# Softmax sums of two attentions inverted by one VectorE reciprocal instead of a logarithm, an exponential and a refinement

## The chip, the cores and the metric

One core of a Trainium2 chip. The metric is the device time of one execution in microseconds (us), the median of several runs; lower is better. Engines: TensorE (PE, matmul; PEld its weight load), VectorE (DVE), ScalarE (ACT), GpSimd (POOL), SyncE (SP, which issues the transfers here).

## The reference

One step of a one-layer encoder over 1024 new prompt frames and 32 sample frames (1056 in all, width 1024): a SwiGLU block, a mixer, a second SwiGLU block, a last norm. The mixer has three groups of columns: a gated convolution, a forgetting attention (8 heads of 64) and a cross-attention over 256 memory tokens (4 heads of 64). Both attentions end in a softmax:

```python
def _mem_attention(q, k, v):
    s = jnp.einsum('bqhd,bkhd->bhqk', q, k).astype(F32) * (HEAD_DIM ** -0.5)
    p = jax.nn.softmax(s, axis=-1)
    return jnp.einsum('bhqk,bkhd->bqhd', p.astype(v.dtype), v)
```

The forgetting attention adds a difference of running sums of log forget values to the logits and masks later keys. Everything is in 32-bit floats. The outputs of the three groups are joined, multiplied by `w_out` and added to x.

## The kernel before, in words

Everything is kept transposed: 128 rows of features by 1056 columns of frames. A matrix product in full precision is three matmuls on parts of each operand (high times high, high times low, low times high; lines 277 to 279). The program is written out by hand for each engine: each engine has its own list of instructions in order, and waits on semaphores that count finished instructions. `A["mixed"]` counts the VectorE instructions that scale the attention's output; TensorE, ScalarE and SP wait for it.

Heads go in pairs of 64 + 64 rows. There are four forgetting pairs (`attend(g)`, about 840 to 1170 us) and two memory pairs (`mem_pairs`, about 1170 to 1271 us), one after the other; then the product with `w_out` (`out_product`) begins. For a pair TensorE makes q, k and v, ScalarE and VectorE norm and split them, TensorE makes scores by row for the row maxima (VectorE, `smax` or `mem_smax`), then scores by key (`keyed`), of which ScalarE takes the exponential (`exps`), then the weighted sum of values (`weigh`, lines 2766 and 3016).

The values of a head stand beside a block of ones of 64 columns (`VO`, `v_and_ones`). So a weighted sum fills a PSUM bank in which 64 rows hold the head's output and the other 64 rows hold the softmax sum, already repeated for every row. Each pair has six such banks, called parts here (x = 0 to 5): for each head two of 512 frames and one of 32.

Each part is scaled as follows. ScalarE (`sum_rough`, lines 1453 and 1455, or `mem_sum_rough`, lines 1619 and 1621) takes the logarithm of the sum from PSUM, then the exponential of its negative: a rough inverse in `lr` (`sum_r0`). VectorE (`mixed`, lines 2217, 2219, 2224, or `mem_mixed`, lines 2314, 2316, 2321) multiplies it by the sum, refines it, and multiplies the output by it into `mixf`. There is one `lr` and one `lt`, so ScalarE waits for the scaling of part x - 1 before it starts on part x.

What stands around it in the order of the engines:

- ScalarE, forgetting pair: `sum_rough(x)` comes among the 28 exponentials, three blocks after the part's last one; copies of turned row maxima (`maxima`, line 1434) follow it.
- VectorE, forgetting pair: all 18 row maxima, then the six parts, then the next pair's head norm (line 1706).
- VectorE, memory pairs: part 0 to 5 of the first pair have row maxima of the second pair between them (`mem_smax(1, ...)`, line 2305); then come two remainders (`mix_lo`, line 2154), and part 0 to 5 of the second pair with a remainder behind each. A remainder is the low part of a row block of the joined output, which `out_product` reads.
- TensorE: a part's bank is free for the next use only after its scaling. In the memory pairs the sums of parts 3, 4 and 5 of the first pair wait for parts 1, 0 and 2 (`mem_bank_free`, line 2991), those of the second pair for parts 3, 4, 5 of the first, and its own part 5 for its own part 2. The output products wait for the banks of the second pair (line 3055).
- SP stores `mixf` after the sixth part of each pair (line 895; line 911 for the first memory pair) and loads the rows back later; `memory_gain` (line 2143) writes over `mixf` after that store.
- ScalarE and VectorE between the fourth forgetting pair and the memory: squares of the memory tokens (line 1518), the tokens' scale (`memory_scaled`, lines 2250 and 2254), the first query's norm, the memory gains (line 2143), for which TensorE waits before its third product (`mp["dve"]`, line 2953).

Of the kernel before, what the change touches and what calls it, by code (L numbers as in the profile page):

```python
# [22 lines left out]
P = 128  # L23
# [8 lines left out]
def hybrid_step(nc, i, o):  # L32
# [31 lines left out]
    with ctx:  # L64
# [120 lines left out]
        lr = sb("sum_r0", [P, 512], F32, xs)  # L185
        lt = sb("sum_rs", [P, 512], F32, xs)
# [48 lines left out]
        def semaphores(tag, names):  # L235
# [14 lines left out]
                       "qhi qlo tturned tcopied scores smax mturned mcopied keyed expd pv rough_sum mixed stored")  # L250
# [185 lines left out]
        def mem_rows(p, i):  # L436
# [5 lines left out]
                         mcopied=5, keyed=MB, expd=MB, pv=MB, rough_sum=12, mixed=18, stored=48)  # L442
# [3 lines left out]
                         mturned=5, mcopied=5, keyed=NB["fox"], expd=NB["fox"], pv=NB["fox"], rough_sum=12, mixed=18,  # L446
# [153 lines left out]
        def _(sp):  # L600
# [283 lines left out]
            for g, (kind, it) in enumerate(ATTEND):  # L884
                v = ITER["conv"] + g
                load_mixer(v + 1)
                store_tokens(g)
                if g + 1 < NG:
                    load_minusF(g + 1)
                    load_cached(g + 1)  # L890
                else:
                    load_mixer(MEMV + 1)
                    load_mem_cached(0)
                sp.wait_ge(A["mixed"], 18 * g + 18)
                store_mix(v)
# [15 lines left out]
            sp.wait_ge(A["mixed"], mem(0, "mixed", 18))  # L911
# [153 lines left out]
        def _(act):  # L1065
# [309 lines left out]
            def last_mix_hi():  # L1375
                act.wait_ge(A["mixed"], mem(1, "mixed", 18))
                act.activation(hh[:, KT - 1, :], mixf[:, :], ACT.Copy).then_inc(MIX["hi_last"], 1)

            def attend(g):
# [116 lines left out]
                done = 0  # L1496
                for n in range(NB[kind]):
                    exps(n)
                    if n == max(V_BEHIND):
                        v_copy(8)  # L1500
                    if n == V_TURNED:
                        tokens(5)
                        tokens(6)
                    if done < 6 and n >= PARTS[kind][done][0] + 3:
                        sum_rough(done)
                        done += 1
# [3 lines left out]
                for x in range(done, 6):  # L1510
                    sum_rough(x)
# [97 lines left out]
            def mem_sum_rough(p, x):  # L1609
                w = mem_block(p, 2 * x)[5]  # L1610
                r = half_rows(1 - x // 3)
                act.wait_ge(A["pv"], mem(p, "pv", 2 * x + 2))
                if x:
                    act.wait_ge(A["mixed"], mem(p, "mixed", 3 * x))
                elif p:
                    act.wait_ge(A["mixed"], mem(0, "mixed", 18))
                else:
                    act.wait_ge(A["mixed"], 18 * NG)
                act.activation(lr[r, 0:w], bank(MEM_OUT[p][x], w)[r], ACT.Ln).then_inc(A["rough_sum"], 1)
                act.wait_ge(A["rough_sum"], mem(p, "rough_sum", 2 * x + 1))  # L1620
                act.activation(lr[r, 0:w], lr[r, 0:w], ACT.Exp, scale=-1.0).then_inc(A["rough_sum"], 1)

            def mem_pairs():
# [34 lines left out]
                for n in range(MB):  # L1658
# [5 lines left out]
                    if n in (4, 6, 8, 10):  # L1664
                        mem_sum_rough(0, n // 2 - 2)
                    if n in (8, 10, 11):
                        mem_maxima(1, (8, 10, 11).index(n))
                mem_sum_rough(0, 4)
                mem_sum_rough(0, 5)
                for n in range(MB):  # L1670
                    mem_exps(1, n)
                    if n in (1, 3):
                        mem_maxima(1, 3 + n // 2)
                    if n in (4, 6, 8, 10):
                        mem_sum_rough(1, n // 2 - 2)
                mem_sum_rough(1, 4)
                mem_sum_rough(1, 5)
# [17 lines left out]
        def _(dve):  # L1695
# [460 lines left out]
            def attend(g):  # L2156
# [54 lines left out]
                def mixed(x):  # L2211
# [97 lines left out]
            def mem_mixed(p, x):  # L2309
# [3 lines left out]
                dve.wait_ge(A["rough_sum"], mem(p, "rough_sum", 2 * x + 2))  # L2313
                dve.tensor_tensor(lt[l, 0:w], PS[l, b:b + w], lr[l, 0:w], ALU.mult).then_inc(A["mixed"], 1)
                dve.wait_ge(A["mixed"], mem(p, "mixed", 3 * x + 1))
                dve.scalar_tensor_tensor(lt[r, 0:w], lt[l, 0:w], -2.0, lr[l, 0:w], ALU.add, ALU.mult)\
                   .then_inc(A["mixed"], 1)
                dve.wait_ge(A["mixed"], mem(p, "mixed", 3 * x + 2))
                if x == 0:
                    dve.wait_ge(MIX["stored"], 16 * (MEMV + p))  # L2320
                dve.scalar_tensor_tensor(mixf[r, s:s + w], PS[r, b:b + w], -1.0, lt[r, 0:w], ALU.mult, ALU.mult)\
                   .then_inc(A["mixed"], 1)
# [63 lines left out]
        def _(pe):  # L2386
# [220 lines left out]
            def attend(g):  # L2607
# [4 lines left out]
                def head_sums(m):  # L2612
# [7 lines left out]
                    elif g and m == 1:  # L2620
                        pe.wait_ge(A["mixed"], 18 * (g - 1) + 9)
# [8 lines left out]
                def bank_free(n):  # L2630
# [6 lines left out]
                    elif g and b in (0, 1, 4, 5):  # L2637
                        pe.wait_ge(A["mixed"], 18 * (g - 1) + {0: 12, 1: 6, 4: 15, 5: 18}[b])
# [115 lines left out]
                def weigh(n):  # L2754
# [7 lines left out]
                    if q0 == SEQ and first:  # L2762
                        pe.wait_ge(A["cv_loaded"], 32 * g + 32)
                        if j:
                            pe.wait_ge(A["mixed"], 18 * g + 3)
# [177 lines left out]
            def mem_product(p, n):  # L2943
# [6 lines left out]
                if p == 0 and n < 2:  # L2950
                    pe.wait_ge(A["mixed"], 18 * (NG - 1) + (6 if n else 12))
# [18 lines left out]
                if (p, n) == (0, 1):  # L2970
                    pe.wait_ge(A["mixed"], 18 * NG)
# [19 lines left out]
            def mem_bank_free(p, x):  # L2991
# [5 lines left out]
                elif p == 0:  # L2997
                    pe.wait_ge(A["mixed"], mem(0, "mixed", (6, 3, 9)[x - 3]))
                elif x < 3:
                    pe.wait_ge(A["mixed"], mem(0, "mixed", (12, 15, 18)[x]))  # L3000
                elif x == 5:
                    pe.wait_ge(A["mixed"], mem(1, "mixed", 9))
# [45 lines left out]
            def out_product(c, d, ks):  # L3048
# [5 lines left out]
                elif ks[0] == 0 and OBANK[d] in (0, 1, 2, 6, 7):  # L3054
                    pe.wait_ge(A["mixed"], mem(1, "mixed", {0: 12, 1: 6, 2: 3, 6: 18, 7: 15}[OBANK[d]]))
# [60 lines left out]
```

## Time and profile before

| | |
|---|---|
| median of 3 runs | 2103.62 us (2102.03 to 2103.83) |
| the profiled execution | 2104.28 us, span 2102.5 us |
| mean granted TensorE clock | 0.988 of full speed |
| TensorE, VectorE, ScalarE, GpSimd busy | 2030.8, 1307.0, 991.0, 451.3 us |
| forgetting pairs | about 840 to 1170 us from the span's start |
| memory pairs | about 1170 to 1271 us |

The profile shows one execution; times count from the span's start. A row of an engine gives the line of the kernel, the operation, out<-in, shapes and durations; in brackets stands for how long the engine was idle before it and what ended that. The product with `w_out` and the two SwiGLU blocks fill most of the rest with matmuls.

### The profile page before, as it was taken

Reading aid. Unit: us, or ns where it says so; the run is one execution under the profiler, and the core shown is the slowest. Engines: PE = TensorE matmul, PEld = TensorE weight load, DVE = VectorE, ACT = ScalarE, POOL = GpSimd, SP = SyncE. Lnnn points to the kernel's source line nnn. Section 1 sums busy time; section 2 is a strip of 40 time slices with the busy share of each in tenths; the row PEclk is TensorE's granted clock in tenths of the full one; section 3 lists DMA queues with packets and bytes.
Section 4 is the critical chain, followed back from the end, with each engine's and each line's share of the span. In section 5 each row is a group of like instructions: output and inputs, shape, how many; then the busy total and the mean of one; then the engine's idle time right before and its main releaser. Section 6 shows DMA issues by size and latency. Waiting matters only on the chain.

```text
span 2102.5 us, 35729 instructions
## 1 busy us (share of the span) xinstructions
PE 2030.8 (97%) x14062; PEld 1935.1 (92%) x14062; DVE 1307.0 (62%) x2087; ACT 991.0 (47%) x1689; POOL 451.3 (21%) x225
## 2 busy tenths in 40 slices
PE   5999999999999999999999979989999999999998
PEld 5999999999999999776877858979999999999997
DVE  7999657983425763645645664589975588723323
ACT  6556344564334431455555652265543456433423
POOL 0000000004666643011012332000000000166662
PEclk8999999999999999999999989999999999999999
DMA  7554324555755447321122133055432265485742
GB/s 230 135 145 132 92 63 143 164 150 186 240 181 188 136 133 51 89 77 46 53 77 54 48 137 130 1 174 160 134 102 82 85 182 162 128 274 173 236 140 113
DMA packets 296853, 274.52 MB, mean 131 GB/s; under 512 B 29864, under 2 KB 238888, under 8 KB 296432
## 3 DMA queue, kind: packets, MB, share of 16 engines
q1 hardware_dynamic: 296688, 272.25, 43.5%
q8 instruction: 113, 1.85, 0.4%
q14 instruction: 52, 0.43, 0.1%
HBM read 222.41 MB, written 49.80 MB: 129 GB/s over the span
## 4 chain that ended last, share of the span: by engine, by line
PE 88%; DVE 5%; ACT 4%; issue 1%; another core or an unknown queue 0%; DVEq 0%; ACTq 0%
PE banks L277 27%; PE banks L278 27%; PE banks L279 26%; PE banks L2766 3%; DVE scores_minusF L2208 1%; PE banks L2734 1%; PE banks L2735 1%; PE banks L2688 1%; ACT k_hi_twice L1400 1%; PE banks L3016 0%; DVE head_rstd L1710 0%; DVE head_rstd L1706 0%; DVE head_rstd L1708 0%; ACT head_r L1088 0%
## 5 line engine op out<-in xcount | busy, mean ns | idle before, releaser
L277 PE MATMUL banks<-hforms_hi,w_hi 128*128 128x264 f32 x2112 | 602.6, 285 | 18.5 <-DVE hforms_lo L1910 9.6
L278 PE MATMUL banks<-hforms_lo,w_hi 128*128 128x264 f32 x2112 | 602.9, 285 | 0.0
L279 PE MATMUL banks<-hforms_hi,w_lo 128*128 128x264 f32 x2112 | 601.5, 285 | 0.0
L968 POOL TENSOR_TENSOR w_lo<-w_raw,w_hi 128x1024 fp32r<-128x1024 f32 x132 | 321.9, 2443 | 1203.2 <-ACT w_hi L1196 1203.2
L277 PEld LDWEIGHTS banks<-hforms_hi,w_hi 128*128 128x128 f32 x2112 | 399.5, 189 | 22.1 <-issue 7.2
L279 PEld LDWEIGHTS banks<-hforms_hi,w_lo 128*128 128x128 f32 x2112 | 398.9, 189 | 0.0
L278 PEld LDWEIGHTS banks<-hforms_lo,w_hi 128*128 128x128 f32 x2112 | 398.5, 189 | 0.1
L277 PE MATMUL banks<-acts_a,w_hi 128*128 128x352 f32 x960 | 309.9, 323 | 0.0
L279 PE MATMUL banks<-acts_a,w_lo 128*128 128x352 f32 x960 | 309.2, 322 | 0.0
L278 PE MATMUL banks<-acts_a,w_hi 128*128 128x352 f32 x960 | 309.0, 322 | 0.0
L1196 ACT ACTIVATE w_hi<-w_raw 128x1024 fp32r<-128x1024 f32 x132 | 139.5, 1058 | 283.1 <-PE banks L279 259.3
L277 PE MATMUL banks<-h_hi,w_hi 128*128 128x352 f32 x576 | 199.6, 347 | 4.8 <-DVE vT L2143 3.0
L279 PE MATMUL banks<-h_hi,w_lo 128*128 128x352 f32 x576 | 187.0, 325 | 0.0
L278 PE MATMUL banks<-h_lo,w_hi 128*128 128x352 f32 x576 | 186.8, 324 | 0.0
L277 PEld LDWEIGHTS banks<-acts_a,w_hi 128*128 128x128 f32 x960 | 180.3, 188 | 0.2
L278 PEld LDWEIGHTS banks<-acts_a,w_hi 128*128 128x128 f32 x960 | 180.3, 188 | 0.2
L279 PEld LDWEIGHTS banks<-acts_a,w_lo 128*128 128x128 f32 x960 | 180.2, 188 | 0.0
L1130 ACT ACTIVATE w_hi<-w_raw 128x512 fp32r<-128x512 f32 x228 | 142.7, 626 | 55.7 <-PE banks L279 53.9
L1130 ACT ACTIVATE w_hi<-w_sums 128x1024 fp32r<-128x1024 f32 x112 | 118.6, 1059 | 87.6 <-PE banks L279 78.5
L1804 DVE TENSOR_TENSOR w_lo<-w_raw,w_hi 128x512 fp32r<-128x512 f32 x228 | 155.8, 683 | 0.1
L1927 DVE TENSOR_TENSOR acts_a<-acts_f,acts_a 128x704 fp32r<-128x704 f32 x60 | 107.1, 1795 | 59.0 <-ACT acts_a L1184 58.9
L1813 DVE TENSOR_TENSOR w_lo<-w_sums,w_hi 128x1024 fp32r<-128x1024 f32 x112 | 136.4, 1218 | 0.4
(338 smaller groups left out, 3557.4 us busy)
## 6 DMA issues: line engine op xcount, KB each, us to landing
w_raw<-in_w_ffn_down SPq DMA_DIRECT2D x132, 512.0 KB, 3.8
w_raw<-in_w_ffn_gate SPq DMA_DIRECT2D x76, 512.0 KB, 5.4
w_raw<-in_w_ffn_up SPq DMA_DIRECT2D x76, 512.0 KB, 5.2
act_rows<-act_f SPq DMA_DIRECT2D x44, 528.0 KB, 2.9
acts_f<-act_rows SPq DMA_DIRECT2D x66, 352.0 KB, 4.1
w_raw<-in_w_in SPq DMA_DIRECT2D x20, 512.0 KB, 5.7
x_spill<-xT SPq DMA_DIRECT2D x4, 2112.0 KB, 8.5
xT<-x_spill SPq DMA_DIRECT2D x6, 1408.0 KB, 9.3
```

The source lines that it names most:

```text
L277: eng.matmul(out, w_hi, x_hi, start=first, stop=False, skip_group_check=added)
L278: eng.matmul(out, w_hi, x_lo, start=False, stop=False, skip_group_check=added)
L279: return eng.matmul(out, w_lo, x_hi, start=False, stop=last, skip_group_check=added)
L968: pool.tensor_tensor(wlo[:, wd_slot(e), :], raw[:, wd_slot(e), :], whi[:, wd_slot(e), :].bitcast(F32), ALU.subtract)\
L1130: act.activation(slots(whi, wxh, G[q], n), src, ACT.Copy).then_inc(f[f"{which}_hi"], 1)
L1196: act.activation(whi[:, wd_slot(e), :], raw[:, wd_slot(e), :], ACT.Copy).then_inc(f["wd_hi"], 1)
L1400: act.activation(KS1[half_rows(j), j, s:s + w], kT[half_rows(j), s:s + w], ACT.Copy)\
L1804: dve.tensor_tensor(slots(wlo, wxl, slot, 1), r[:, at:at + 1, :], slots(whi, wxh, slot, 1).bitcast(F32), ALU.subtract).then_inc(f[f"{which ...
L1813: dve.tensor_tensor(slots(wlo, wxl, slot, 2), SS[:, 2 * part:2 * part + 2, :], slots(whi, wxh, slot, 2).bitcast(F32), ALU.subtract)\
L1927: dve.tensor_tensor(acts(p)[:, 1, :, :], astg[:, m % 4, :, :], acts(p)[:, 0, :, :].bitcast(F32), ALU.subtract).then_inc(f["act_lo"], 1)
L2208: dve.tensor_tensor_reduce(junk[0:rows, 0:w], PS[0:rows, b:b + w], nF[0:rows, j, k0:k0 + w], 1.0, -3e38, ALU.add, ALU.max, m).then_inc(A[" ...
L2766: pe.matmul(PS[:, 512 * ob + oc:512 * ob + oc + w], VO[0:kr, vo, j, :], PRT[0:kr, (b0 + n) % 4, 0:w], start=first, stop=last, skip_group_c ...
```

## The change

One VectorE reciprocal per part takes the place of ScalarE's two instructions and VectorE's first two. It reads the sums from PSUM and writes their inverse into the output's rows of `lt`, which has two halves used in turn. The part's wait is for TensorE's last weighted sum (`A["pv"]`) in place of ScalarE's. ScalarE's `sum_rough` and `mem_sum_rough` and their waits are gone; `lr` is gone. `A["mixed"]` counts two instructions per part instead of three, and every wait on it is renumbered to the same part.

```diff
-        lr = sb("sum_r0", [P, 512], F32, xs)
-        lt = sb("sum_rs", [P, 512], F32, xs)
+        lt = sb("one_over_sums", [P, 2, 512], F32, xs)
...
-                def sum_rough(x):
-                    n, j, b, w, s = PARTS[kind][x]
-                    r = half_rows(1 - j)
-                    act.wait_ge(A["pv"], b0 + n + 1)
-                    act.wait_ge(A["mixed"], 18 * g + 3 * x)
-                    at = 2 * (6 * g + x)
-                    act.activation(lr[r, 0:w], bank(b, w)[r], ACT.Ln).then_inc(A["rough_sum"], 1)
-                    act.wait_ge(A["rough_sum"], at + 1)
-                    act.activation(lr[r, 0:w], lr[r, 0:w], ACT.Exp, scale=-1.0).then_inc(A["rough_sum"], 1)
...
-                    at = 18 * g + 3 * x
-                    dve.wait_ge(A["rough_sum"], 2 * (6 * g + x) + 2)
-                    dve.tensor_tensor(lt[l, 0:w], PS[l, b:b + w], lr[l, 0:w], ALU.mult).then_inc(A["mixed"], 1)
-                    dve.wait_ge(A["mixed"], at + 1)
-                    dve.scalar_tensor_tensor(lt[r, 0:w], lt[l, 0:w], -2.0, lr[l, 0:w], ALU.add, ALU.mult)\
-                       .then_inc(A["mixed"], 1)
-                    dve.wait_ge(A["mixed"], at + 2)
+                    dve.wait_ge(A["pv"], b0 + n + 1)
+                    dve.reciprocal(lt[r, x % 2, 0:w], PS[l, b:b + w]).then_inc(A["mixed"], 1)
+                    dve.wait_ge(A["mixed"], 2 * (6 * g + x) + 1)
                     if x == 0:
                         dve.wait_ge(MIX["stored"], 16 * (ITER["conv"] + g))
-                    dve.scalar_tensor_tensor(mixf[r, s:s + w], PS[r, b:b + w], -1.0, lt[r, 0:w], ALU.mult, ALU.mult)\
-                       .then_inc(A["mixed"], 1)
+                    dve.tensor_tensor(mixf[r, s:s + w], PS[r, b:b + w], lt[r, x % 2, 0:w], ALU.mult).then_inc(A["mixed"], 1)
...
-                dve.wait_ge(A["rough_sum"], mem(p, "rough_sum", 2 * x + 2))
...
+                dve.wait_ge(A["pv"], mem(p, "pv", 2 * x + 2))
+                dve.reciprocal(lt[r, x % 2, 0:w], PS[l, b:b + w]).then_inc(A["mixed"], 1)
+                dve.wait_ge(A["mixed"], mem(p, "mixed", 2 * x + 1))
...
+                dve.tensor_tensor(mixf[r, s:s + w], PS[r, b:b + w], lt[r, x % 2, 0:w], ALU.mult).then_inc(A["mixed"], 1)
```

## Rows read from the trace of the kernel before

**Rows 1.** The page, part 1: busy time of each engine, share of the span, instructions.

```profile
PE 2030.8 (97%) x14062; PEld 1935.1 (92%) x14062; DVE 1307.0 (62%) x2087; ACT 991.0 (47%) x1689; POOL 451.3 (21%) x225
```

**Rows 2.** Table by windows of 10 us: busy us of each engine (instructions), PEclk, DMA.

```profile
910.00:920.00 10.00, 10.00 (x47) 6.00 (x47) 1.92 (x8) 6.46 (x16) 0.00 (x0) 1.00 0.01 2
1180.00:1190.00 10.00, 6.97 (x35) 6.27 (x33) 4.28 (x11) 3.58 (x6) 5.09 (x3) 0.83 0.00 1
1240.00:1250.00 10.00, 9.59 (x36) 6.11 (x34) 4.83 (x8) 3.57 (x8) 9.92 (x8) 0.72 0.27 91
1250.00:1260.00 10.00, 6.59 (x21) 3.77 (x22) 7.72 (x12) 4.28 (x10) 1.91 (x2) 0.83 0.21 70
```

**Rows 3.** Waits between 1220 and 1300 us: us in total, times, longest.

```profile
ACT sum_r L1619 <- DVE mix_f L2321: 14.8, 10, 2.3
...
PE banks L3016 <- DVE mix_f L2321: 4.6, 1, 4.6
```

**Rows 4.** Instructions of the two tiles of the inversion: ns minimum, median, maximum.

```profile
L2314 DVE TENSOR_TENSOR sum_rs<-banks,sum_r x12: 182/684/695, 1232.6 to 1277.4; 64x512 f32<-64x512 f32 x8, 64x32 f32<-64x32 f32 x4
L2316 DVE SCALAR_TENSOR_TENSOR sum_rs<-sum_rs,sum_r x12: 184/685/1458, 1233.3 to 1277.6; 64x512 f32<-64x512 f32 x8, 64x32 f32<-64x32 f32 x4
L2321 DVE SCALAR_TENSOR_TENSOR mix_f<-banks,sum_rs x12: 182/682/695, 1234.8 to 1277.8; 64x512 f32<-64x512 f32 x8, 64x32 f32<-64x32 f32 x4
...
L1619 ACT ACTIVATE sum_r<-banks x12: 191/591/597, 1231.3 to 1276.9; 64x512 f32<-64x512 f32 x8, 64x32 f32<-64x32 f32 x4
L1621 ACT ACTIVATE sum_r<-sum_r x12: 226/626/632, 1231.9 to 1277.1; 64x512 f32<-64x512 f32 x8, 64x32 f32<-64x32 f32 x4
```

**Rows 5.** Groups by line and shape, and one line's instructions: a cast, a scan.

```profile
L2280 DVE CAST k_hi_twice<-kT 64x512 fp32r<-64x512 f32 x4 | 1.7, 422 | 0.1
...
L2082 DVE TENSOR_TENSOR_SCAN F_rows<-f_ones,logf_rows x2: 453/1366/2280, 838.0 to 840.2; 8x1024 f32<-8x1024 f32 x1, 8x160 f32<-8x160 f32 x1
```

**Rows 6.** TensorE's waits from 840 to 1220 us; ScalarE in time order.

```profile
PE banks L2703 <- issue: 3.1, 4, 0.8
...
900.94 0.63 ACT L1455 ACTIVATE sum_r<-sum_r 64x512 f32<-64x512 f32 x1
901.59 0.59 ACT L1434 ACTIVATE q_hi_and_max<-banks 1x512 fp32r<-1x512 f32 x1
```

**Rows 7.** End of the first forgetting pair in time order: TensorE, then VectorE.

```profile
915.60 0.86 PE L2766 MATMUL banks<-probsT,v_and_ones 128*128 128x384 f32 x2
...
918.76 2.45 PE L2766 MATMUL banks<-probsT,v_and_ones 128*128 128x512 f32 x6
...
924.40 0.69 DVE L2224 SCALAR_TENSOR_TENSOR mix_f<-banks,sum_rs 64x512 f32<-64x512 f32 x1
928.72 0.52 DVE L1706 SCALAR_TENSOR_TENSOR head_rstd<-banks,head_r 128x352 f32<-128x352 f32 x1 [3.63 <-ACT head_r L1090]
```

**Rows 8.** The turn to the memory pairs in time order: VectorE, then TensorE.

```profile
1174.20 0.17 DVE L2250 TENSOR_SCALAR tiny<-tiny 128x2 f32<-128x2 f32 x1
...
1181.47 1.65 DVE L2143 TENSOR_SCALAR vT<-banks,gains 128x256 f32<-128x256 f32 x4
...
1183.26 0.40 PE L277 MATMUL banks<-h_hi,w_hi 128*128 128x352 f32 x1 [3.03 <-DVE vT L2143]
```

**Rows 9.** The memory pairs in time order: VectorE, then TensorE.

```profile
1231.65 0.68 DVE L2305 TENSOR_REDUCE row_max<-banks 32x2 f32<-32x512 f32 x1 [1.06 <-PE banks L2866]
...
1245.01 0.69 DVE L2305 TENSOR_REDUCE row_max<-banks 128x2 f32<-128x512 f32 x1 [2.29 <-PE banks L2866]
...
1269.58 0.18 DVE L2321 SCALAR_TENSOR_TENSOR mix_f<-banks,sum_rs 64x32 f32<-64x32 f32 x1
1269.69 1.24 DVE L2154 TENSOR_TENSOR h_lo<-h_lo,h_hi 128x1056 fp32r<-128x1056 f32 x1
...
1239.51 2.04 PE L3016 MATMUL banks<-probsT,v_and_ones 128*128 128x512 f32 x2 [4.64 <-DVE mix_f L2321]
...
1271.49 0.40 PE L277 MATMUL banks<-h_hi,w_hi 128*128 128x352 f32 x1
```

More of the change, by code:

```diff
@@ L249, in hybrid_step @@
         A = semaphores("att", "ck_loaded cv_loaded minusF_loaded proj squares sums rough nrm vcopied cturned past khi kdve "
-                       "qhi qlo tturned tcopied scores smax mturned mcopied keyed expd pv rough_sum mixed stored")
+                       "qhi qlo tturned tcopied scores smax mturned mcopied keyed expd pv mixed stored")
         s_init = sem("attention_constants")
@@ L441, in hybrid_step @@
                          past=1, khi=2, kdve=4, qhi=12, qlo=6, tturned=2, tcopied=2, scores=MR, smax=MR, mturned=5,
-                         mcopied=5, keyed=MB, expd=MB, pv=MB, rough_sum=12, mixed=18, stored=48)
+                         mcopied=5, keyed=MB, expd=MB, pv=MB, mixed=12, stored=48)
         FOX_COUNT = dict(ck_loaded=16, cv_loaded=32, proj=NPROJ["fox"], squares=NSQ["fox"], sums=NSQ["fox"],
@@ L445, in hybrid_step @@
                          kdve=4 * NKP["fox"], qhi=12, qlo=6, tturned=NTT["fox"], tcopied=NTT["fox"], scores=18, smax=18,
-                         mturned=5, mcopied=5, keyed=NB["fox"], expd=NB["fox"], pv=NB["fox"], rough_sum=12, mixed=18,
+                         mturned=5, mcopied=5, keyed=NB["fox"], expd=NB["fox"], pv=NB["fox"], mixed=12,
                          stored=NSTORED["fox"])
@@ L893, in _ @@
                     load_mem_cached(0)
-                sp.wait_ge(A["mixed"], 18 * g + 18)
+                sp.wait_ge(A["mixed"], 12 * g + 12)
                 store_mix(v)
@@ L910, in _ @@
                 load_w_out(b)
-            sp.wait_ge(A["mixed"], mem(0, "mixed", 18))
+            sp.wait_ge(A["mixed"], mem(0, "mixed", 12))
             store_mix(MEMV)
@@ L1375, in last_mix_hi @@
             def last_mix_hi():
-                act.wait_ge(A["mixed"], mem(1, "mixed", 18))
+                act.wait_ge(A["mixed"], mem(1, "mixed", 12))
                 act.activation(hh[:, KT - 1, :], mixf[:, :], ACT.Copy).then_inc(MIX["hi_last"], 1)
@@ L1503, in attend @@
                         tokens(6)
-                    if done < 6 and n >= PARTS[kind][done][0] + 3:
-                        sum_rough(done)
-                        done += 1
                     for h in range(2):
@@ L1509, in attend @@
                             maxima(3 + h)
-                for x in range(done, 6):
-                    sum_rough(x)
             def memory_rough():
@@ L1607, in mem_exps @@
                 act.activation(PRT[:, n % 4, 0:w], bank(MEM_S[n % 2], w), ACT.Exp).then_inc(A["expd"], 1)
[L1609 to L1621, printed above, removed]
             def mem_pairs():
@@ L2620, in head_sums @@
                     elif g and m == 1:
-                        pe.wait_ge(A["mixed"], 18 * (g - 1) + 9)
+                        pe.wait_ge(A["mixed"], 12 * (g - 1) + 6)
                     pe.matmul(bank(6 + m % 2, w), onesH[:, :], hsq[:, m % 2, 0:w], start=True, stop=True)\
@@ L2637, in bank_free @@
                     elif g and b in (0, 1, 4, 5):
-                        pe.wait_ge(A["mixed"], 18 * (g - 1) + {0: 12, 1: 6, 4: 15, 5: 18}[b])
+                        pe.wait_ge(A["mixed"], 12 * (g - 1) + {0: 8, 1: 4, 4: 10, 5: 12}[b])
                     elif g == 0 and n < 5:
@@ L2764, in weigh @@
                         if j:
-                            pe.wait_ge(A["mixed"], 18 * g + 3)
+                            pe.wait_ge(A["mixed"], 12 * g + 2)
                     pe.matmul(PS[:, 512 * ob + oc:512 * ob + oc + w], VO[0:kr, vo, j, :], PRT[0:kr, (b0 + n) % 4, 0:w],
@@ L2950, in mem_product @@
                 if p == 0 and n < 2:
-                    pe.wait_ge(A["mixed"], 18 * (NG - 1) + (6 if n else 12))
+                    pe.wait_ge(A["mixed"], 12 * (NG - 1) + (4 if n else 8))
                 elif p == 0:
@@ L2970, in mem_product @@
                 if (p, n) == (0, 1):
-                    pe.wait_ge(A["mixed"], 18 * NG)
+                    pe.wait_ge(A["mixed"], 12 * NG)
                     turn_memory()
@@ L2997, in mem_bank_free @@
                 elif p == 0:
-                    pe.wait_ge(A["mixed"], mem(0, "mixed", (6, 3, 9)[x - 3]))
+                    pe.wait_ge(A["mixed"], mem(0, "mixed", (4, 2, 6)[x - 3]))
                 elif x < 3:
-                    pe.wait_ge(A["mixed"], mem(0, "mixed", (12, 15, 18)[x]))
+                    pe.wait_ge(A["mixed"], mem(0, "mixed", (8, 10, 12)[x]))
                 elif x == 5:
-                    pe.wait_ge(A["mixed"], mem(1, "mixed", 9))
+                    pe.wait_ge(A["mixed"], mem(1, "mixed", 6))
                 else:
@@ L3054, in out_product @@
                 elif ks[0] == 0 and OBANK[d] in (0, 1, 2, 6, 7):
-                    pe.wait_ge(A["mixed"], mem(1, "mixed", {0: 12, 1: 6, 2: 3, 6: 18, 7: 15}[OBANK[d]]))
+                    pe.wait_ge(A["mixed"], mem(1, "mixed", {0: 8, 1: 4, 2: 2, 6: 12, 7: 10}[OBANK[d]]))
                 for k in ks:
```

16 lines of the change are left out of this document (removed).

## The prediction

> **What bounds the kernel now.** I read the page first. TensorE is busy for 97% of the span, VectorE for 62%, ScalarE for 47% [rows 1]. So removed work pays only where TensorE stands still for it. Next I read the table by windows, to find such places. Inside a forgetting pair TensorE is full (910 to 920 us: busy 10.00 of 10.00 at full clock); in the memory pairs it is not (6.59 of 10 us between 1250 and 1260), and there the granted clock drops too, to 0.72 and 0.83 on average [rows 2]. Third, the waits of that stretch. TensorE waited 4.6 us in one piece for a VectorE result of the softmax scaling, and ScalarE waited 14.8 us in ten pieces for the same line before it could start the next inversion [rows 3]. The memory pairs are therefore paced by a loop in which ScalarE and VectorE hand one buffer back and forth. That is the place where this change decides.
>
> **The change, part by part.** It removes two ScalarE instructions and two VectorE instructions per part of the output and adds one reciprocal. There are 24 parts in the four forgetting pairs and 12 in the two memory pairs; two thirds are 512 columns wide, one third 32.
> Old price of a 512-wide part: 0.59 + 0.63 us on ScalarE, then 3 x 0.68 us on VectorE, about 3.3 us in sequence. The middle VectorE step took up to 1.46 us in this stretch [rows 4]. New price on VectorE: R for the reciprocal, 0.68 us for the product, 0.07 us of gaps. ScalarE pays nothing.
>
> R is in no row. A pass over the columns costs (684 - 182) / 480 = 1.046 ns a column and 0.15 us fixed, from the product's two widths [rows 4]. The cheapest near row is a cast of 64x512 at 0.42 us. The nearest form, one that reads PSUM and writes SBUF, is the product at 0.68. The dearest per column is the scan, (2280 - 453) / 864 = 2.1 ns, which would make 1.2 us of 512 columns [rows 5]. But all of these do one addition, product or comparison per element. A quotient of 24 bits is developed in steps, and if one pass over the datapath yields three bits, eight passes are needed. That count is my choice, not a reading: R = 8 x 512 x 1.046 + 150 ns = 4.43 us, and 0.42 us for 32 columns. I keep one pass (0.68 us) as the other end.
> The Trainium skill (VectorE: DVE Perf Modes, section Walkthrough: the 8-slice pipeline in each mode) says that the reciprocal is an iterative divide with a repeat count of 8; by that rule the sum is the one below. No row here shows it.
>
> Step 1, the forgetting pairs. ScalarE's removed work sits in front of a copy of the row maxima (901.59 starts when the inversion that began at 900.94 is through), and TensorE idles 0.8 us for that copy once in each of four pairs, 3.1 us in all [rows 6]. I take back 0.6 us each: **-2.4 us**. VectorE has nothing else to do there after its maxima. Does it still finish? Part 4's last accumulation is the matmul from 915.60 (to 916.5), part 5's the last of those from 918.76 (to 921.2). At 5.2 us each they end at 921.7 and 926.9, instead of 925.1 now; VectorE's next job, the head norm, starts at 928.72 [rows 7]. Slack 1.8 us: nothing lost. Without that slack each 1 us over would move the next pair's norms. Banks 4 and 5, which they hold longer, are wanted by the next pair's fifth and sixth product only. SP's store of the mixed rows comes as much later as part 5, with nothing urgent behind it.
>
> Step 2, the turn from the fourth forgetting pair to the memory. There VectorE goes straight on: part 5 ends 1.8 us later, so the scaling of the memory tokens (1174.20 now) does as well. Behind it in order stand the ScalarE roots, the squares of the first query, their norm, and the memory gains, which end at 1183.1 and for which TensorE already stands still 3.03 us [rows 8]. The squares have about 0.5 us of slack before TensorE wants them: **+1.3 us**.
>
> Step 3, the memory pairs. The first row maximum ends at 1232.3. VectorE then does part 0 (5.2), two maxima (1.3), part 1 (5.2): 1244.0. TensorE's accumulation of part 3 waits for part 1 and starts at 1239.51 now [rows 9]: +4.5 us. From there to the end of the fifth maximum VectorE follows TensorE as now (1245.7, so 1250.2). Then VectorE's own queue, with no help from anybody, sets the pace. Part 2 of the first pair 0.7; a maximum with its wait 1.1; part 3 5.2; two maxima 1.3; part 4 5.2; a maximum and part 5 1.4; two remainders of 1.25; part 0 of the second pair 5.2; remainder 1.25; part 1 5.2; remainder 1.25; part 2 0.7. Together 31.0, so 1281.2. The same point is 1269.8 now, and the last bank of the second pair waits for it; the output products, which start at 1271.49 now [rows 9], start at 1281.5: +10.0. Before that TensorE will have stood still for some 8 us, twice before for 9 and 4 us. After its standstills of today it ran on the lower of its two clock levels (1.2 instead of 2.4 GHz): a mean of 0.83 in the window after the 3 us wait at 1180, so 3.4 us at half speed and 1.7 us of work lost, and 0.72 after the 4.6 us wait, 2.8 us lost [rows 2, 8, 9]. One such loss falls into the output products: +2.2. Bank 7 for the seventh of them is free at 1294.1 and wanted at 1295.3, so no further wait. Together **+12.2 us**.
>
> What is moved costs nothing else. SP's store of the first memory pair and the reload behind it end before 1275, and the split of that row block is wanted only after 1290. The second buffer is paid by nobody and waited for by nobody, because one engine writes and reads it in order.
>
> Sum: -2.4 + 1.3 + 12.2 = +11.1 us on the profiled execution's 2104.28 us, 2115.4. That execution lies 0.7 us over the median of 2103.62, so the forecast is **2115 us**.
>
> **Rivals.**
> *One pass.* The reciprocal costs what the product beside it costs, 0.68 us. For it: every VectorE row of this width lies between 0.42 and 0.7 us. Against: none of them divides. Its place is VectorE's queue between the first and the last part of the memory pairs, its price 6.7 us of the time per us of R (25.0 us between the two sums, over 3.75 us), and it decides below R = 2.8 us, where the sum is nought. A part then takes 1.45 us: TensorE resumes at 1236.5 (-3.0), a standstill of 2 us instead of 4.6, so the 2.8 us at half clock go too. The queue of step 3 shrinks from 31.0 to 15.3, so it would end at 1258.0. But TensorE and the exponentials need until about 1260: -11.5. With step 1 unchanged and step 2 nought: 2104.3 - 13.9 = 2090.4, as a median **2090 us**. The Trainium skill (Vector Engine (DVE) Microarchitecture Reference, section Anatomy of a single slice) describes the divide as a chain that spans all eight slices; if a new element can enter that chain every cycle, it is this rival.
> *Few passes, or a standstill on both sides.* At four to six passes (R from 2.3 to 3.3 us) that slope gives -3 to +3.6 us: the change trades ScalarE's share and the handing back and forth for the same time on VectorE. That is also where a wait that takes the place of another would show: TensorE's 4.6 us on part 1 stay about as they are. **2104 us**.
> *More clock than priced.* With eight passes, if each of the three standstills costs 2.8 us at half speed on the path: 2115 + 5, **2120 us**. It counts as the slow case.
> *The change does not do what it says.* The inversion could still wait for ScalarE. The diff leaves no such wait; 1 in 100, inside the middle case.
>
> **How the numbers follow.** Eight passes or nearly so, slower: 0.58. The middle case: 0.12. One or two passes, faster: 0.30, since neighbours in the trace speak for it. These are my three chances; what counts as no change is a move within 0.2%, 4.2 us, about what a measurement of this kernel can tell. The slow case's own range is 2108 to 2121 (from R = 3.4 us to the clock rival). Leaving the fast case out would drop 3 in 10, so the range must reach it: 2089 to 2121.
>
> **What would show it.** The reciprocal's own row decides: 4.4 us for 64x512 and 0.4 for 64x32, or 0.7. Then: TensorE's wait in the memory pairs for the second part near 9 us at 1244, or 2 us; a new wait of about 8 us just before the output products at 1281, or none. The 3.1 us of the forgetting pairs shrink below 1 in either case. The turn to the memory: TensorE's 3.03 us become about 4.3, or stay. The forecast is wrong if the reciprocal's row is under 2.8 us, and wrong in step 1 if the head norm that now starts at 928.72 starts later than the squares allow.

## The result, and the profile after

Over 17 runs each, the changed kernel takes 2106.25 us (2104.06 to 2107.22) and the kernel before 2102.03 us (2100.64 to 2105.49). The ratio is 1.0019, with a 95% interval of 1.0012 to 1.0026: slower by 4.2 us. The interval excludes a ratio of 1, though 0.19% is just short of the 0.2% below which the prediction spoke of no change. The forecast was +11.1 us (2115 us against a median of 2103.62): direction right and time within the range, but the size is off by 7 us.

The profiled execution took 2106.73 us (span 2104.9), against 2104.28 us (span 2102.5) before: only +2.4 us, since single executions scatter.

The page's first part, after, answers to [rows 1]. The work left ScalarE and came to VectorE; TensorE's share stayed.

```profile
PE 2032.4 (97%) x14062; PEld 1940.2 (92%) x14062; DVE 1345.7 (64%) x2051; ACT 958.2 (46%) x1617; POOL 451.1 (21%) x225
```

The instructions that write the tile of the inverses, after (ns minimum, median, maximum; first and last start; forms). They take the place of [rows 4].

```profile
L2177 DVE RECIPROCAL one_over_sums<-banks x24: 350/3350/3360, 899.3 to 1166.3; 64x512 f32<-64x512 f32 x16, 64x32 f32<-64x32 f32 x8
L2270 DVE RECIPROCAL one_over_sums<-banks x12: 351/3352/3360, 1228.4 to 1282.0; 64x512 f32<-64x512 f32 x8, 64x32 f32<-64x32 f32 x4
L2274 DVE TENSOR_TENSOR mix_f<-banks,one_over_sums x12: 183/682/695, 1231.8 to 1282.4; 64x512 f32<-64x512 f32 x8, 64x32 f32<-64x32 f32 x4
```

This is the row the prediction called decisive. R is **3.35 us**, not the 4.43 us that I assumed and not the 0.68 us of one pass. From both widths it costs (3352 - 351) / 480 = 6.25 ns a column, six times the 1.046 ns of the product under it. The count of eight passes was too high.

The waits after, 1220 to 1310 us (us in total, times, longest), answer to [rows 3].

```profile
PE banks L2968 <- DVE mix_f L2274: 11.4, 2, 7.6
PE banks L2818 <- DVE row_max L2261: 3.3, 1, 3.3
PE banks L2940 <- ACT probsT L1590: 2.2, 1, 2.2
```

TensorE's one standstill of 4.6 us on the softmax scaling became two (7.6 and 3.8 us), and a third of 3.3 us on a row maximum that stood behind a reciprocal in VectorE's queue. ScalarE's ten waits for the buffer are gone.

The same stretch in time order, after, VectorE and then TensorE (start, us, engine; in brackets the idle time before), answers to [rows 9].

```profile
1227.71 0.68 DVE L2261 TENSOR_REDUCE row_max<-banks 32x2 f32<-32x512 f32 x1 [1.05 <-PE banks L2818]
1228.42 3.36 DVE L2270 RECIPROCAL one_over_sums<-banks 64x512 f32<-64x512 f32 x1
...
1237.94 1.19 PE L2968 MATMUL banks<-probsT,v_and_ones 128*128 128x512 f32 x1 [7.59 <-DVE mix_f L2274]
...
1250.07 0.80 PE L2818 MATMUL banks<-k_hi_twice,second_q_hi_lo 128*128 128x256 f32 x2 [3.26 <-DVE row_max L2261]
...
1269.70 1.03 PE L2968 MATMUL banks<-probsT,v_and_ones 128*128 128x32 f32 x4 [3.78 <-DVE mix_f L2274]
1270.54 0.64 PE L276 MATMUL banks<-h_hi,w_hi 128*128 128x352 f32 x1
```

Compare three points with before. The first row maximum starts at 1227.71 instead of 1231.65: the change arrives here 3.9 us early. The output products start at 1270.54 instead of 1271.49: 0.9 us early, so the memory pairs gave back 3.0. The execution ends 2.4 us late, so 3.4 us more went behind that point. The table by windows after has two places with a lower clock (columns as in [rows 2]):

```profile
1230.00:1240.00 10.00, 2.41 (x5) 1.05 (x4) 7.70 (x6) 0.97 (x3) 9.76 (x7) 0.75 0.64 191
...
1260.00:1270.00 10.00, 6.22 (x25) 3.73 (x23) 9.83 (x9) 2.78 (x6) 2.29 (x1) 0.96 0.28 98
1270.00:1280.00 10.00, 10.00 (x48) 10.00 (x48) 9.87 (x5) 2.95 (x3) 8.03 (x3) 0.70 0.84 329
...
1370.00:1380.00 10.00, 6.00 (x27) 5.49 (x28) 7.15 (x9) 7.67 (x9) 0.00 (x0) 0.58 1.03 357
```

And the same two late windows before the change:

```profile
1270.00:1280.00 10.00, 9.40 (x59) 9.05 (x58) 8.14 (x12) 5.47 (x10) 1.63 (x1) 1.00 0.80 316
...
1370.00:1380.00 10.00, 5.81 (x33) 5.60 (x34) 5.65 (x8) 7.25 (x11) 0.00 (x0) 0.83 1.02 353
```

Between 1260 and 1270 VectorE is busy for 9.8 of 10 us and TensorE for 6.2: VectorE is the bound there, as forecast. After the 3.8 us standstill TensorE starts the output products at a mean granted clock of 0.70 (before: 1.00). With two levels, 1.2 and 2.4 GHz, that is 6 us at the lower one and 3.0 us of work lost. In the window from 1370 it is 0.58 against 0.83.

How much of the 3.4 us each place costs is read from two later starts of TensorE that both traces have, before and then after:

```profile
1368.78 0.39 PE L277 MATMUL banks<-hforms_hi,w_hi 128*128 128x264 f32 x1 [1.68 <-DVE hforms_lo L1910]
...
1389.90 0.39 PE L277 MATMUL banks<-hforms_hi,w_hi 128*128 128x264 f32 x1 [1.28 <-DVE w_lo L1804]
```

```profile
1370.29 0.39 PE L276 MATMUL banks<-hforms_hi,w_hi 128*128 128x264 f32 x1 [1.67 <-DVE hforms_lo L1871]
...
1392.13 0.39 PE L276 MATMUL banks<-hforms_hi,w_hi 128*128 128x264 f32 x1 [1.25 <-DVE w_lo L1765]
```

From the start of the output products to the first of these is 97.3 us before and 99.8 after: 2.5 us, the lower clock at the start of those products. From there to the second is 21.1 and 21.8 us: 0.7 us. So the low clock from 1370 costs little.

### The profile page after: what moved, and what is told of

Read it like the earlier page. It is cut to its first block, busy times and chain, and to the rows that moved or that the text cites. A ratio compares the mean times of both kernels' runs of the same rounds, so it can differ in the third digit from the quotient of the medians.

```text
span 2104.9 us, 35585 instructions
## 1 busy us (share of the span) xinstructions
PE 2032.4 (97%) x14062; PEld 1940.2 (92%) x14062; DVE 1345.7 (64%) x2051; ACT 958.2 (46%) x1617; POOL 451.1 (21%) x225
## 4 chain that ended last, share of the span: by engine, by line
PE 88%; DVE 5%; ACT 3%; issue 1%; another core or an unknown queue 0%; DVEq 0%; ACTq 0%
PE banks L276 27%; PE banks L277 27%; PE banks L278 26%; PE banks L2718 3%; DVE scores_minusF L2169 1%; DVE one_over_sums L2270 1%; PE banks L2686 1%; PE banks L2687 1%; PE banks L2640 1%; ACT k_hi_twice L1399 1%; PE banks L2968 0%; DVE head_rstd L1671 0%; DVE head_rstd L1669 0%; DVE head_rstd L1667 0%
```

## The experiments

Theory after the result: three things add up. The forgetting pairs gain some 4 us. In the memory pairs VectorE's queue sets the end, at about 6 us per us of R. The lower clock after the standstills adds to that. The rivals are named in each expectation. Where no count is given, 5 runs of the kernel stand against 15 of the kernel before on the same chip. The ratio is worked out from all the runs and can differ by 0.1% from the quotient of the two medians given beside it; gains and losses in us go by the ratio.

**The reciprocal in the forgetting pairs alone.** The memory pairs keep logarithm, exponential, refinement and one buffer (they use the two halves of the new one as the old two tiles).

```diff
 (memory pairs, ScalarE)
+                act.activation(lt[r, 1, 0:w], bank(MEM_OUT[p][x], w)[r], ACT.Ln).then_inc(A["rough_sum"], 1)
+                act.activation(lt[r, 1, 0:w], lt[r, 1, 0:w], ACT.Exp, scale=-1.0).then_inc(A["rough_sum"], 1)
 (memory pairs, VectorE)
-                dve.reciprocal(lt[r, x % 2, 0:w], PS[l, b:b + w]).then_inc(A["mixed"], 1)
+                dve.tensor_tensor(lt[l, 0, 0:w], PS[l, b:b + w], lt[l, 1, 0:w], ALU.mult).then_inc(A["mixed"], 1)
...
```

> Only the 24 parts of the forgetting pairs use the reciprocal; the memory pairs keep logarithm, exponential and refinement. Theory: the change pays in the forgetting pairs, because ScalarE's queue loses two instructions per part and VectorE has room; the trace after shows the memory pairs starting 3.9 us earlier, so this kernel is 4 us faster than before (ratio 0.998). Rival: the 3.35 us reciprocal delays the next pair's norm or the token turn and the gain is an accident of two traces: no difference or up to 2 us slower.

Measured: 2099.38 us (11 runs) against 2104.43; ratio 0.9983 (0.9975 to 0.9992). This half gains 3.6 us, as the theory had it. Waits of TensorE between 840 and 1220 us in this run: the 3.1 us in four pieces of [rows 6] have no row any more.

```profile
PE banks L2666 <- DVE row_max L2191: 4.4, 16, 0.4
PE banks L276 <- DVE vT L2126: 3.0, 1, 3.0
PE banks L276 <- DVE row_max L2191: 1.8, 4, 0.4
PE banks L2600 <- ACT head_squares L1466: 1.5, 2, 1.3
```

**The reciprocal in the memory pairs alone**, where the two old tiles serve as the two buffers; the forgetting pairs are as before.

```diff
 (memory pairs, VectorE; ScalarE's two activations fall away)
+                dve.reciprocal((lt, lr)[x % 2][r, 0:w], PS[l, b:b + w]).then_inc(A["mixed"], 1)
...
```

> Only the 12 parts of the memory pairs use the reciprocal. Theory: VectorE's queue is the bound there, five wide parts in it before the last bank comes free, so this kernel carries the whole loss and none of the saving: about 8 us slower than before (ratio 1.0038), with a standstill of TensorE near 7.5 us at the first wait and near 4 us before the output products. Rival: the memory pairs cost only what the two kernels differ by, 4 us (ratio 1.002), and the forgetting pairs save nothing.

Measured: 2113.51 us against 2104.43; ratio 1.0045 (1.0033 to 1.0058). This half costs 9.4 us (6.9 to 12.2): the theory's 8 us lies within, the rival's 4 us does not. Its waits between 1220 and 1310 us are those of the whole change:

```profile
PE banks L2990 <- DVE mix_f L2296: 11.2, 2, 7.6
PE banks L2840 <- DVE row_max L2283: 3.3, 1, 3.3
```

The product of the two ratios, 0.9983 x 1.0045 = 1.0028, lies by the whole change's 1.0019 (0.0009 above, which is within the two intervals).

**Nothing but a pass.** Both reciprocals are replaced by copies of the same operands; the outputs are then multiplied by their sums instead of divided.

```diff
-                dve.reciprocal(lt[r, x % 2, 0:w], PS[l, b:b + w]).then_inc(A["mixed"], 1)
+                dve.tensor_copy(lt[r, x % 2, 0:w], PS[l, b:b + w]).then_inc(A["mixed"], 1)
```

> The kernel after with a plain copy of the sums in place of every reciprocal, so the output is multiplied by the sum and not divided by it. It prices the rival of one pass. Theory: the time falls by the reciprocal's excess, about 2.7 us per wide part at 6.7 us per us: about 14 to 16 us under before (near 2087, ratio 0.993), and TensorE's first standstill shrinks to about 2 us. Rival: below some price TensorE and the exponentials are the bound and the saving ends at about 6 us under before (ratio 0.997).

Measured: 2090.44 us against 2104.43; ratio 0.9926 (0.9911 to 0.9941). This is the one-pass rival as a kernel: its price in the prediction was 2090 us. In the trace the copy takes 684 ns. TensorE stands still for 2.2 us (the prediction had 2), and the output products start 27.7 us after the first row maximum of the memory pairs (1257.70 and 1229.98), where the prediction's points make 28.4.

```profile
L2270 DVE COPY one_over_sums<-banks x12: 183/684/693, 1230.7 to 1264.1; 64x512 f32<-64x512 f32 x8, 64x32 f32<-64x32 f32 x4
```

**A longer inversion.** A second reciprocal of 256 columns goes into the buffer that is free just then; the added wait keeps it behind the product that reads that buffer.

```diff
 (memory pairs, VectorE)
+                if w == 512:
+                    if x or p:
+                        dve.wait_ge(A["mixed"], mem(p, "mixed", 2 * x))
+                    dve.reciprocal(lt[r, (x + 1) % 2, 0:256], PS[l, b:b + 256])
                 dve.reciprocal(lt[r, x % 2, 0:w], PS[l, b:b + w]).then_inc(A["mixed"], 1)
```

> Changed kernel, with a second reciprocal of 256 columns (into the buffer that is free just then) ahead of the reciprocal of every 512-wide part of the two memory pairs. By the row of this reciprocal (6.25 ns per column and 0.15 us) it adds 1.75 us to each of these parts, so R goes from 3.35 to 5.1 us. Theory (VectorE's queue between the first and the last part of the memory pairs sets the end, 6.7 us of the time per us of R): 1.75 x 6.7 = +11.7 us over the changed kernel, about 2118 us, and a ratio to the kernel before of 1.0075. Rival (the standstills of the changed kernel have other causes, for example the late first row maximum or the transfers of that stretch, and the reciprocal is only part of it): +3 us or less over the changed kernel, ratio below 1.0035.

Measured: 2117.7 us against 2105.54; ratio 1.0057 (1.0044 to 1.0070). The rival is out, yet 1.0075 was too much as well: over the changed kernel it is 1.0057 - 1.0019 = 0.0038, or 8 us. The added row is right, and the last accumulation of the memory pairs starts 10.0 us later than in the changed kernel (1280.3 against 1270.3); six reciprocals of 1.75 us in the queue make 10.5.

```profile
L2273 DVE RECIPROCAL one_over_sums<-banks x8: 1750/1752/1760, 1228.9 to 1287.9; 64x256 f32<-64x256 f32 x8
```

The clock did not get worse along with it: 0.69 in the window from 1280, where its output products start, as against 0.70 in the changed kernel. The stretch that has 0.58 from 1370 there comes 10 us later here, with the same 0.58:

```profile
1380.00:1390.00 10.00, 5.94 (x27) 5.43 (x28) 7.21 (x9) 7.67 (x9) 0.00 (x0) 0.58 1.02 358
```

**Half of the inversion**, then **three quarters** (384 in place of 256).

```diff
 (memory pairs, VectorE)
-                dve.reciprocal(lt[r, x % 2, 0:w], PS[l, b:b + w]).then_inc(A["mixed"], 1)
+                dve.reciprocal(lt[r, x % 2, 0:min(w, 256)], PS[l, b:b + min(w, 256)]).then_inc(A["mixed"], 1)
```

> Changed kernel, with the reciprocal of every 512-wide part of the two memory pairs cut to its first 256 columns; for the other 256 the product reads what the buffer held before, so half of these outputs are not divided by their sums. R falls from 3.35 to 1.75 us there. Theory (6.7 us of the time per us of R, break-even with the kernel before near R = 2.8 us in the whole, lower where only the memory pairs are looked at): 1.6 x 6.7 = -10.7 us against the changed kernel, about 2095.5 us, ratio 0.9965. Rival (the slope flattens as soon as VectorE's queue is shorter than TensorE's and the exponentials' work, so most of the gain is already had at half of this cut): 2090 to 2092 us, ratio 0.993 to 0.994, as in the run without a reciprocal.

Measured: 2096.07 us against 2105.54; ratio 0.9951 (0.9939 to 0.9964). The gain on the changed kernel, 1.0019 - 0.9951 = 0.0068 or 14 us, lies between theory and rival. The queue explains 6 x 1.6 = 9.6 us (the last accumulation starts at 1259.9, 10.4 earlier). The rest is clock: TensorE's longest wait on the scaling is 4.4 us instead of 7.6, and the output products run at 1.00 from the start, at 1260.02 (the second of the two rows below). From there to the end it takes 831.3 us, and 834.4 in the changed kernel.

```profile
L2270 DVE RECIPROCAL one_over_sums<-banks x12: 351/1752/1760, 1228.3 to 1267.5; 64x256 f32<-64x256 f32 x8, 64x32 f32<-64x32 f32 x4
```

```profile
1260.00:1270.00 10.00, 10.00 (x64) 10.00 (x64) 9.74 (x9) 4.84 (x5) 8.21 (x3) 1.00 0.95 377
```

> Changed kernel, with the reciprocal of every 512-wide part of the two memory pairs cut to 384 columns; for the other 128 the product reads what the buffer held before, so a quarter of these outputs are not divided by their sums. R = 0.15 + 384 x 0.00625 = 2.55 us instead of 3.35. Set out from the last accumulation of the memory pairs, which starts at 1280.2 with R = 5.1, at 1270.3 with 3.35 and at 1259.9 with 1.75, about 6 us per us of R: 1265.2 here. Theory (VectorE's queue alone, in proportion): 0.8 x 6.5 = -5.2 us against the changed kernel, ratio about 0.9995, so the break-even with the kernel before lies just above 2.55 us. Rival (a second term, the lower clock after the long standstills, comes and goes in one step: the half-length run was 3 us faster than the queue explains): if the 4 us or so of lower clock ahead of and in the output products are already gone here, -8 us, ratio 0.998.

Measured: 2102.88 us (11 runs) against 2105.68 (17); ratio 0.9992 (0.9983 to 1.0000). Theory 0.9995, within the interval; the rival's 0.998 is just outside.

```profile
L2270 DVE RECIPROCAL one_over_sums<-banks x12: 351/2551/2560, 1233.0 to 1279.4; 64x384 f32<-64x384 f32 x8, 64x32 f32<-64x32 f32 x4
```

The expectation's 1265.2 for the last accumulation came out as 1270.9, because this execution entered the memory pairs 4.6 us late. From the first to the last accumulation it took 45.3 us, and 48.9 in the changed kernel (mean of two executions): -3.6 us.

**The changed kernel once more**, beside the three quarters; nothing is edited.

> The changed kernel once more, on the chip and beside the runs of the next kernel, so that the two can be set against each other directly. Both theories: a ratio to the kernel before of 1.0019, between 1.0012 and 1.0035.

Measured: 2109.85 us (7 runs) against 2105.68; ratio 1.0024 (1.0012 to 1.0035). Same chip, direct: three quarters against whole is 2102.88 to 2109.85, -7.0 us. The queue explains 6 x 0.8 = 4.8 of it, and the rival had -8: so part of the clock's loss goes already here (1270 to 1280 us at 0.83, after 0.70 and 0.74 in the two executions of the changed kernel; from the output products' start to the end 832.7 us after 834.4 in both), and the two theories are not told apart by this step alone.

The seven runs by R in the memory pairs. The last two columns are from the profiled executions: the stretch from the first to the last accumulation there, and the time from the first row maximum there to the end of the span, which holds the clock behind the stretch as well:

| R, 512 columns | kernel | ratio | stretch, us | row maximum to end, us |
|---|---|---|---|---|
| 0.68 (copy, also in the forgetting pairs) | nothing but a pass | 0.9926 | 33.9 | 859.5 |
| 1.75 | half | 0.9951 | 38.7 | 863.7 |
| 2.55 | three quarters | 0.9992 | 45.3 | 871.5 |
| 3.35 | the change, twice | 1.0019, 1.0024 | 49.3, 48.5 | 877.2, 876.8 |
| 3.35 | memory pairs alone | 1.0045 | 49.5 | 877.5 |
| 5.10 | longer | 1.0057 | 58.7 | 887.0 |

From 1.75 to 5.10 us of R the stretch grows by 20.0 us, 6.0 per us, and the last column by 23.3, 7.0 per us; the prediction had 6.7. The ratio passes 1 between 2.55 and 3.35; in proportion, at 2.55 + 0.8 x 8 / (8 + 21.5) = 2.8 us, counting 0.0008 below and a mean of 0.00215 above. The interval at 2.55 reaches up to 1.0000, so the crossing can lie as low as 2.55.

**The old scheme with a second buffer** for the rough inverse in the memory pairs. The buffer is a tile that is otherwise unused there. With it come two further waits: VectorE's for its own last product before each part, and one of GpSimd for the last scaling, before a low part of `w_out`, where it stands for 2.1 us.

```diff
 (memory pairs, ScalarE; VectorE reads the same buffer)
-                if x:
-                    act.wait_ge(A["mixed"], mem(p, "mixed", 3 * x))
+                if x > 1:
+                    act.wait_ge(A["mixed"], mem(p, "mixed", 3 * x - 3))
...
-                act.activation(lr[r, 0:w], bank(MEM_OUT[p][x], w)[r], ACT.Ln).then_inc(A["rough_sum"], 1)
+                act.activation((lr, junk)[x % 2][r, 0:w], bank(MEM_OUT[p][x], w)[r], ACT.Ln).then_inc(A["rough_sum"], 1)
```

> Kernel before, with a second buffer for the rough inverse in the two memory pairs alone: ScalarE may begin the next part's logarithm while VectorE still refines the last one. The instructions and their number stay. Theory (in the memory pairs the hand-back of the one buffer is what ScalarE waits 14.8 us for and what holds TensorE's 4.6 us): the inversion of the next part, 1.2 us, is ready when VectorE comes to it, TensorE's 4.6 us shrink to about 3, and the time falls by 2 to 5 us, ratio about 0.998. Rival (ScalarE's waits are slack, the order of ScalarE's own instructions and the exponentials pace the stretch): no change, ratio 0.9995 to 1.0005.

Measured: 2101.57 us (11 runs) against 2105.54; ratio 0.9981 (0.9973 to 0.9990), a gain of 4.0 us. The size is the theory's, its way is not. Waits between 1220 and 1310 us:

```profile
PE banks L3020 <- DVE mix_f L2325: 5.4, 2, 4.6
PE banks L2992 <- ACT probsT L1609: 2.8, 3, 2.2
ACT scores_minusF L1621 <- DVE mix_f L2325: 2.6, 2, 2.0
```

And the row of the kernel before that answers to the second:

```profile
PE banks L2988 <- ACT probsT L1607: 5.7, 4, 2.2
```

(The tile scores_minusF is the second buffer.) ScalarE stands 2.6 us for a buffer instead of 14.8 [rows 3], and so comes to its exponentials sooner: TensorE's wait for these falls from 5.7 us to 2.8. The 4.6 us on the scaling stay (5.4 us in all, from 4.6). So these waits give 2.1 of the 4.0 us; where the rest comes from is not shown. VectorE's time order says why the 4.6 us stay:

```profile
1238.06 0.68 DVE L2325 SCALAR_TENSOR_TENSOR mix_f<-banks,sum_rs 64x512 f32<-64x512 f32 x1
1238.67 1.27 DVE L2307 TENSOR_REDUCE row_max<-banks 128x2 f32<-128x512 f32 x2
1239.97 0.69 DVE L2318 TENSOR_TENSOR sum_rs<-banks,scores_minusF 64x512 f32<-64x512 f32 x1
1240.70 1.20 DVE L2320 SCALAR_TENSOR_TENSOR sum_rs<-sum_rs,scores_minusF 64x512 f32<-64x512 f32 x1
1241.93 0.68 DVE L2325 SCALAR_TENSOR_TENSOR mix_f<-banks,sum_rs 64x512 f32<-64x512 f32 x1
```

There is no gap: what ends TensorE's wait at 1242.76 is VectorE's own work, not the hand-back. In the kernel before the hand-back was little more: 0.18 us ahead of the same part.

```profile
1236.86 0.69 DVE L2314 TENSOR_TENSOR sum_rs<-banks,sum_r 64x512 f32<-64x512 f32 x1 [0.18 <-ACT sum_r L1621]
```

**Both gains together**: reciprocal in the forgetting pairs, old scheme with two buffers in the memory pairs (the first and the last edit above).

> Reciprocal in the four forgetting pairs alone, logarithm, exponential and refinement in the memory pairs, there with two buffers for the rough inverse in turn. Theory (the gains add): the forgetting pairs give 4 us, the second buffer what the run beside this one shows for it, 2 to 5 us; together 2097 us, ratio 0.996 to 0.997. Rival (the second buffer brings nothing): as with the reciprocal in the forgetting pairs alone, ratio 0.998.

Measured: 2098.72 us against 2105.54; ratio 0.9965 (0.9951 to 0.9978). The gains add. By the ratios this version beats the kernel before by 0.35%, 7.4 us (6.8 by the medians), and the changed one by 0.54%.

## Why the prediction was right in direction and wrong in size

**The reciprocal's price.** This is the step that failed. The prediction took R = 4.43 us from a count of eight passes that it called "my choice, not a reading"; the row says 3.35, which is what six passes make by the same sum (6 x 512 x 1.046 + 150 ns = 3.36 us). The working was meant to carry any R: 6.7 us of the time per us of R. With 1.08 us less that is -7.2, and +11.1 becomes +3.9, against +4.2 measured. The mechanism in the memory pairs, VectorE's queue, was right; the term for the reciprocal was a third too large. One reading of the opening did not hold: that the 4.6 us standstill came from the hand-back of the one buffer. It stays at 4.6 us with two buffers.

The Trainium skill (VectorE: DVE Perf Modes, section Walkthrough: the 8-slice pipeline in each mode) gives the divide a repeat count of 8. The trace does not show eight passes of the product's pace, but 6.25 / 1.046 = 6.0. The Trainium skill (Vector Engine (DVE) Microarchitecture Reference, section Anatomy of a single slice) describes the divide as a chain that spans all eight slices. The rival's reading of it, one new element per cycle at the price of a product, is refuted by the same row: 3.35 us and not 0.68.

**Step 1, the forgetting pairs: right, a little small.** Forecast -2.4 us. The products of the scaling, before and after:

```profile
L2224 DVE SCALAR_TENSOR_TENSOR mix_f<-banks,sum_rs x24: 183/682/695, 903.0 to 1173.4; 64x512 f32<-64x512 f32 x16, 64x32 f32<-64x32 f32 x8
```

```profile
L2181 DVE TENSOR_TENSOR mix_f<-banks,one_over_sums x24: 181/682/695, 902.7 to 1169.7; 64x512 f32<-64x512 f32 x16, 64x32 f32<-64x32 f32 x8
```

From the first to the last it took 270.4 us, and takes 267.0: -3.4. I had left 0.2 us of each 0.8 us standstill; all of it went. Measured alone, -3.6 us (-5.3 to -1.7).

**Step 2, the turn to the memory: did not come.** Forecast +1.3. It rested on part 5 ending 1.8 us later, which at the measured R is 1.8 - 2 x 1.08 = -0.4. TensorE waits 3.03 us as before:

```profile
1179.35 0.40 PE L276 MATMUL banks<-h_hi,w_hi 128*128 128x352 f32 x1 [3.03 <-DVE vT L2104]
```

**Step 3, the memory pairs: right in form.** With the earlier start (-3.9) and the smaller R, the prediction's own points can be checked. Its first standstill ends at 1244.0 - 3.9 - 2 x 1.08 = 1237.9; measured 1237.94. The output products start at 1281.5 - 3.9 - 6 x 1.08 = 1271.1; measured 1270.54. So the count of VectorE's queue holds to 0.6 us. The clock was under-priced: 2.2 forecast, 3.4 seen behind the start of the output products. Alone, this half costs 9.4 us (6.9 to 12.2) where steps 2 and 3 with the true R give 13.5 - 7.2 = 6.3. So the corrected sum of +3.9 comes as near to +4.2 as it does because two errors partly cancel, which is luck: 1.2 us too little gain in step 1 (within that run's interval) and 3.1 too little loss here (just outside it).

Where the 3.1 us come from can be read in the traces. From the first row maximum of the memory pairs to the end, the reciprocal there takes 877.2, 876.8 and 877.5 us. The old inversion takes 870.9 us in the profiled execution that the prediction was worked from, and 868.1 in the kernel with the reciprocal in the forgetting pairs alone, whose instructions there are the same:

```profile
1227.87 0.68 DVE L2283 TENSOR_REDUCE row_max<-banks 32x2 f32<-32x512 f32 x1 [1.05 <-PE banks L2844]
```

```profile
1240.00:1250.00 10.00, 6.23 (x37) 4.34 (x35) 8.84 (x14) 4.49 (x11) 8.12 (x7) 1.00 0.10 39
1250.00:1260.00 10.00, 8.27 (x33) 4.92 (x33) 7.01 (x11) 7.02 (x15) 1.05 (x1) 1.00 0.46 162
```

Its TensorE waits 4.6 us on the scaling as well, but its clock in these two windows is 1.00, and 0.72 and 0.83 in [rows 2]. Against 868.1 the reciprocal costs 8.7 to 9.4 us, as the runs have it. So the base of the prediction held 2.8 us that the old inversion does not always take, and the clock in these windows is the difference that the traces show.

**The rivals.** *One pass* is refuted as a fact and confirmed as a price (2090 forecast, 2090.44 measured). *Few passes* had four to six passes, R from 2.3 to 3.3 us and -3 to +3.6 us. Six passes make 3.36 us and +3.9: it is what happened, at its upper end. It had the smallest chance, 0.12. Its sentence that TensorE's 4.6 us would stay as they are was wrong: 7.6. *More clock*: the clock is low after each of the three standstills (0.75, 0.73 and 0.70 in the windows from 1230, 1250 and 1270), but only the third costs time behind the start of the output products, 2.5 us. The break-even forecast, R = 2.8 us, agrees with the interpolation above.

Left open: how the two profiled stretches from 1370 come to 0.58 and 0.83 of the clock. The transfers there look alike (share 1.03 and 1.02). The four executions with the whole reciprocal or more in the memory pairs have 0.58, 0.54, 0.52 and 0.58 in that stretch; the others have 0.70 to 0.83.

## What to carry to other kernels

Before moving an inversion to VectorE, price it at 6.25 ns per column and 0.15 us fixed for 64 partitions from PSUM (3.35 us for 512), and count how many stand in one queue between the work TensorE waits for: here six, so each microsecond cost six, and with the clock behind it seven. Fewer instructions are no gain where the engine that bounds the stretch gets more time (here 3.35 + 0.68 us a part on VectorE against 3 x 0.68). The same edit can gain in one stage and lose in the next: split it by stage, and look whether the old scheme only lacked a second buffer.

## What the runs showed that was not expected

**The reciprocal is linear in its columns at six times the product's price**: 0.35, 1.75, 2.55 and 3.35 us for 32, 256, 384 and 512 columns.

**The same standstill does not always cost the same clock.** The changed kernel was profiled twice. Each time TensorE stood 3.0 us at the turn to the memory. The windows of the first execution, then of the second:

```profile
1175.00:1180.00 5.00, 1.97 (x17) 1.76 (x15) 4.17 (x10) 1.89 (x3) 1.20 (x1) 1.00 0.00 0
1180.00:1185.00 5.00, 5.00 (x22) 4.50 (x21) 0.30 (x1) 1.35 (x3) 3.49 (x2) 0.66 0.00 0
```

```profile
1175.00:1180.00 5.00, 3.09 (x25) 2.83 (x23) 4.32 (x10) 1.54 (x4) 0.00 (x0) 1.00 0.00 0
1180.00:1185.00 5.00, 3.88 (x23) 3.70 (x24) 0.97 (x3) 2.61 (x4) 4.43 (x2) 1.00 0.00 0
```

One fell to 0.66, the other stayed at 1.00. The kernel with the old inversion in the forgetting pairs needed 51.5, 52.7 and 52.7 us from its last scaling there to the first accumulation of the memory pairs in three executions, the changed one 51.3 and 50.1. The memory pairs of two executions with the same instructions there differed by 2.8 us (870.9 and 868.1, above). So a point of one trace against the same point of another is good to 1 to 3 us, and effects of that size have to come from repeated runs.

**One remainder took 2.99 us instead of 1.24** in the changed kernel, at 1274.86, while GpSimd was busy for 8.03 of 10 us. It took 3.02 in its second execution and 2.99 with the reciprocal in the memory pairs alone. VectorE's steps that touch no PSUM had gone up to 1.46 us before [rows 4], there too while GpSimd was at work (9.04 of 10 us from 1230). That GpSimd is the cause was not tested.

```profile
L2115 DVE TENSOR_TENSOR h_lo<-h_lo,h_hi x7: 1240/1249/2994, 1256.1 to 1282.6; 128x1056 fp32r<-128x1056 f32 x7
```
